# A 128-row score product with the forget bias in the free half of the key remainder

## The reference, cut to what matters

```python
log_f = jax.nn.log_sigmoid(f_logits.astype(jnp.float32) + b_f.astype(jnp.float32))
F = jnp.cumsum(log_f, axis=1).transpose(0, 2, 1)
s = jnp.einsum('bqhd,bkhd->bhqk', qc, k).astype(jnp.float32) * scale
s = s + Fq[..., None] - F[:, :, None, :]
```

## Time and profile before

| | |
|---|---|
| median of three runs | 1847.43 us |
| span of the profiled execution (first to last instruction) | 1849.7 us |
| busy: PE, DVE, ACT, POOL | 96%, 57%, 47%, 8% of the span |
| mean granted TensorE clock | 0.979 |

### The profile page before, as it was taken

How to read it: one execution, slowest core, us unless ns; L and a number is a source line. 1 busy time by engine, 2 the same in 40 slices (tenths; PEclk the granted TensorE clock), 3 DMA queues, 4 the chain that set the end, 5 groups by cost and what they waited for, 6 DMA issues and landing times.

```text
span 1849.7 us, 26742 instructions
## 1 busy us (share of the span) xinstructions
PE 1781.5 (96%) x8160; PEld 1344.1 (73%) x8160; DVE 1059.8 (57%) x2636; ACT 867.4 (47%) x1841; POOL 144.1 (8%) x170
## 2 busy tenths in 40 slices
PE   5999999999999999999969999999999999999997
PEld 3767777777777777888847777777777777688885
DVE  6467777765545555333465777777555554543344
ACT  3566666654444444222236666665444444432222
POOL 3121111100000000000023111111000000000000
PEclk8989999999999999999979999999999999999998
DMA  7220101012212123333432101011112221233331
GB/s 187 61 58 24 35 24 35 24 44 56 63 46 65 49 57 103 92 101 95 121 102 68 35 24 35 24 35 35 47 46 69 51 63 46 57 122 94 99 94 68
DMA packets 223875, 118.05 MB, mean 64 GB/s; under 512 B 20128, under 2 KB 220832, under 8 KB 223264
## 3 DMA queue, kind: packets, MB, share of 16 engines
q1 hardware_dynamic: 219104, 107.66, 21.8%
q0 software_dynamic: 1216, 8.65, 1.2%
q10 hardware_dynamic: 3456, 0.54, 0.2%
HBM read 110.41 MB, written 6.42 MB: 63 GB/s over the span
## 4 chain that ended last, share of the span: by engine, by line
PE 80%; ACT 7%; DVE 7%; issue 4%; POOL 1%; ACTq 1%; DVEq 0%; POOLq 0%
PE acc L1295 51%; PE o_pair L1381 9%; PE scores L1345 6%; PE turned L1358 5%; PE scores L1344 3%; ACT kk_hi L701 2%; PE scores L1349 2%; ACT w_hi L646 2%; ACT q_swap L682 1%; ACT prob L763 1%; DVE w_lo L929 1%; PE o_pair L1411 1%; PE misc L1396 1%; PE turned L1467 1%; DVE prob L1046 1%
## 5 line engine op out<-in xcount | busy, mean ns | idle before, releaser
L1295 PE MATMUL acc<-h_hi,w_hi 128*128 128x512 f32 (+1 forms) x1152 | 473.4, 411 | 30.0 <-DVE h_lo L431 24.1
L1295 PE MATMUL acc<-h_hi,w_lo 128*128 128x512 f32 (+1 forms) x1152 | 465.3, 404 | 0.0
L1295 PE MATMUL acc<-h_lo,w_hi 128*128 128x512 f32 (+1 forms) x1152 | 463.5, 402 | 0.0
L763 ACT ACTIVATE prob<-prob,row_max 128x128 f32<-128x128 f32 (+3 forms) x384 | 214.8, 559 | 270.1 <-DVE row_max L1027 268.1
L929 DVE TENSOR_TENSOR w_lo<-w_raw,w_hi 128x1024 fp32r<-128x1024 f32 x192 | 233.5, 1216 | 147.0 <-ACT w_hi L646 144.4
L1295 PEld LDWEIGHTS acc<-h_hi,w_hi 128*128 128x128 f32 (+1 forms) x1152 | 215.8, 187 | 101.8 <-DVE h_lo L431 29.4
L646 ACT ACTIVATE w_hi<-w_raw 128x1024 fp32r<-128x1024 f32 x192 | 199.7, 1040 | 180.2 <-PE acc L1295 176.1
L1295 PEld LDWEIGHTS acc<-h_hi,w_lo 128*128 128x128 f32 (+1 forms) x1152 | 216.1, 188 | 65.4 <-issue 21.4
L1295 PEld LDWEIGHTS acc<-h_lo,w_hi 128*128 128x128 f32 (+1 forms) x1152 | 216.3, 188 | 56.5 <-issue 16.1
L1027 DVE CUSTOM_DVE_ANT_0 prob<-scores,causal 128x128 f32<-128x128 f32 (+3 forms) x384 | 186.3, 485 | 118.3 <-PE scores L1349 55.0
L772 ACT ACTIVATE pt_hi<-turned 128x128 fp32r<-128x128 f32 (+3 forms) x384 | 165.1, 430 | 174.2 <-PE turned L1358 169.9
(11 more groups left out here) (156 smaller groups left out, 2066.4 us busy)
## 6 DMA issues: line engine op xcount, KB each, us to landing
w_raw<-in_w_in_dram SPq DMA_DIRECT2D x140, 512.0 KB, 3.8
w_raw<-in_w_proj_nsa_dram SPq DMA_DIRECT2D x16, 512.0 KB, 3.6
w_raw<-in_w_proj_fox_dram SPq DMA_DIRECT2D x16, 512.0 KB, 3.6
w_raw<-in_w_out_dram SPq DMA_DIRECT2D x16, 512.0 KB, 3.5
x_scratch<-xT POOLq DMA_DIRECT2D x2, 2048.0 KB, 9.2
xT<-x_scratch POOLq DMA_DIRECT2D x2, 2048.0 KB, 8.2
x_nat<-in_x_dram SPq DMA_DIRECT2D x2, 1024.0 KB, 6.7
c_w<-in_cmp_w_k_dram SPq DMA_DIRECT2D x4, 512.0 KB, 7.6
```

The lines of the kernel that those rows point to most:

```text
L763: act.activation(prob[:, ring, 0:width], prob[:, ring, 0:width], ACT.Exp, bias=row_max[:, ring:ring + 1], scale=-1.0, accum_out=row_sum[:, ...
L1295: ins = pe.matmul(acc[par][0:width, :], w[:, par, k, 0:width], rhs, start=(n == 0), stop=(n == 23))
```

## The change

`q_st` gets one more axis of two: index 0 is as before; index 1 is for fox and holds the rounded query in `own(h)` and, in `other(h)`, two rows of ones and 62 rows of zeros. `kk_lo[other(h)]` holds for fox the two bias rows and zeros. The second score matmul then has 128 rows: for fox index 1 by all of `kk_lo`; for NSA index 0, the same weights as the first, by all of `kk_lo`. The third matmul, `sel`, `sel_f` and `f_row` go. `q_round` writes the rounded fox query twice with one instruction. POOL clears the free half of `kk_lo` at the change from NSA to fox, once per buffer and layer, and fetches two rows per head with a transfer each. The ones and zeros of `q_st` are written once, at the start; so `q_st` moves to a place that nothing else overlays.

```diff
-        sel_f = sb("sel_f", [36, 2, P])
-        sel = sb("sel", [36, 2, P], F32R)
+        q_st = sb("q_st", [P, 2, 2, 2, T], F32R)
...
-            q_st = sb("q_st", [P, 2, 2, T], F32R)
+            sb("place_of_c_hid", [P, 4, T])
...
-            f_row = sb("f_row", [36, T], F32R)
...
-            pool.memset(sel_f[:, :, :], 1.0).then_inc(consts, 1)
+            pool.memset(q_st[:, :, :, 1, :].rearrange("p b h t -> p (b h) t").bitcast(F32), 0.0).then_inc(consts, 1)
...
-            for b in range(2):
-                rows = sel_f[32 * b:32 * b + 4]
...
+            for h in range(2):
+                first = HD * (1 - h)
+                pool.wait_ge(consts, 9 + h)
+                pool.memset(q_st[first:first + 2, :, h, 1, :].bitcast(F32), 1.0).then_inc(consts, 1)
...
-                    pool.dma_start(f_row[32 * proj.b:32 * proj.b + 4, :],
-                                   f_dram[bass.ds(2 * proj.i, 2)].rearrange("h a t -> (h a) t")
-                                   ).then_inc(f_landed, 16)
+                    if prev.nsa:
+
+                        if att.nsa:
+                            pool.wait_ge(cmp_pool, 3 * (att.l * PAIRS + att.i) + 3)
+                            apart(pool)
+                        for h in range(2):
+                            pool.memset(kk_lo[other(h), proj.b, h, :].bitcast(F32), 0.0).then_inc(bias_rows, 1)
+                        pool.wait_ge(bias_rows, 4 * l + 2 * proj.b + 2)
+                        apart(pool)
+                    for h in range(2):
+                        first = HD * (1 - h)
+                        pool.dma_start(kk_lo[first:first + 2, proj.b, h, :],
+                                       f_dram[bass.ds(2 * proj.i + h, 1)].rearrange("h a t -> (h a) t")
+                                       ).then_inc(f_landed, 16)
...
+                    if with_bias:
+                        ins = act.activation(q_st[own(h), b, h, :, :],
+                                             src[own(h), :].unsqueeze(1).broadcast_to([HD, 2, T]), ACT.Copy)
+                    else:
+                        ins = act.activation(q_st[own(h), b, h, 0, :], src[own(h), :], ACT.Copy)
...
-                    pe.matmul(to, q_st[:, pair.b, h, cols], kk_hi[:, b, stream, 0:n], start=True, stop=False)
-                    ins = pe.matmul(to, q_st[own(h), pair.b, h, cols], kk_lo[own(h), b, stream, 0:n], start=False,
-                                    stop=branch is not None)
-                    if branch is None:
-                        rows = slice(32 * b, 32 * b + 4)
-                        ins = pe.matmul(to, sel[rows, h, :], f_row[rows, 0:n], start=False, stop=True)
+                    pe.matmul(to, q_st[:, pair.b, h, 0, cols], kk_hi[:, b, stream, 0:n], start=True, stop=False)
+                    ins = pe.matmul(to, q_st[:, pair.b, h, 1 if branch is None else 0, cols],
+                                    kk_lo[:, b, stream, 0:n], start=False, stop=True)
```

More of the change, by code:

```diff
@@ L370, in bass_trunk @@
         z_done = sem("z_done")
-        sel_done = sem("sel_done")
+        bias_rows = sem("bias_rows")
         y_mul = sem("y_mul")
@@ L389, in bass_trunk @@
         kv_widths = [w for _, w in KV_UNITS]
-        N_CONSTS = 14
+        N_CONSTS = 12
         def apart(eng):
@@ L537, in _ @@
                                channel_multiplier=1).then_inc(consts, 1)
-            for b in range(2):
-                rows = sel_f[32 * b:32 * b + 4]
[L541 to L546, removed]
+            for h in range(2):
+                first = HD * (1 - h)
+                pool.wait_ge(consts, 9 + h)
+                pool.memset(q_st[first:first + 2, :, h, 1, :].bitcast(F32), 1.0).then_inc(consts, 1)
+            pool.wait_ge(consts, 11)
             pool.affine_select(out=past_first[:, :], in_=past_first[:, :], compare_op=ALU.is_ge, fill=0.0,
@@ L684, in swap_copy, with q_round @@
                     ins.then_inc(swap_done, 1)
-            def q_round(src, b, waits, heads=(0, 1)):
+            def q_round(src, b, waits, heads=(0, 1), with_bias=False):
                 for s, value in waits:
@@ L690, in q_round @@
                 for h in heads:
-                    ins = act.activation(q_st[own(h), b, h, :], src[own(h), :], ACT.Copy)
+                    if with_bias:
[3 more added lines that the diff above has]
+                        ins = act.activation(q_st[own(h), b, h, 0, :], src[own(h), :], ACT.Copy)
                 if 1 in heads:
@@ L752, in body @@
                         v_waits = [(cmp_s, PAIRS * (l + 1))] if att.nsa else [(v_turned, n)]
-                        at(plan.at_end(0, 1), lambda: q_round(acc[0], proj.b, q_waits))
+                        at(plan.at_end(0, 1), lambda: q_round(acc[0], proj.b, q_waits, with_bias=True))
                         at(plan.at_end(1, 1), lambda: k_round(acc[1], places, k_waits))
@@ L970, in q_rest @@
                 for h in range(2):
-                    ins = dve.tensor_tensor(q_st[other(h), b, h, :], src[own(h), :], q_st[own(h), b, h, :],
+                    ins = dve.tensor_tensor(q_st[other(h), b, h, 0, :], src[own(h), :], q_st[own(h), b, h, 0, :],
                                             ALU.subtract)
@@ L1112, in _ @@
             dve.wait_ge(consts, N_CONSTS)
-            dve.tensor_copy(sel[:, :, :], sel_f[:, :, :]).then_inc(sel_done, 1)
             for k in range(KT):
@@ L1339, in score_step @@
                         if not pair.nsa:
-                            pe.wait_ge(f_landed, 16 * (pair.l * PAIRS + pair.i + 1))
+                            pe.wait_ge(f_landed, 32 * (pair.l * PAIRS + pair.i + 1))
                     if s >= 2 or prev is not None or pair is not att:
@@ L1449, in _ @@
                 ins.then_inc(x_turned, 1)
-            pe.wait_ge(sel_done, 1)
             sum_squares(0)
```

## The result

The changed kernel takes 1718.6 us, median of four runs (1717.1 to 1719.5); the kernel before took 1848.7 us on the same chip. The ratio is 0.9304 [0.9289, 0.9320]. The profiled execution has a span of 1717.8 us, 131.9 less than before.

What follows compares the result with a forecast made beforehand. PE's matmuls were taken as the bound, with DVE's 28.7 us as floor of an NSA body. Fox 63 + 9 and NSA 46 + 11 gave 129 us off 1847.4: 1718 us, own range 1703 to 1738, wider range 1680 to 1766.

Steps and rivals of the forecast that it cites:

- The price of a step: PE time saved per score step: 0.39 us in NSA; 0.69, 0.76 or 0.83 us in fox for 256, 384, 512 columns.
- The fox body: Saves 5.94 us on PE, loses 1.45 in slots 4 and 5, so gains 4.5, to about 33.1 us.
- The NSA body: Saves 6.24 us on PE but gains 3.3 after waits, mostly for DVE, to about 34.3 us.
- slots 8 to 12: NSA stretch where the chain runs through ACT and DVE and keeps its length: four steps, 1.56 us, gain nothing.
- slots 4 to 6: NSA slots where DVE also has gated output and compressed-branch sums between its steps: estimated 0.9 us late.
- The mixed bodies: Two NSA bodies that project fox queries: PE stays their bound, 6.5 us gain at most, 5.5 taken each.
- The last fox bodies: Two bodies with seven score steps and a chain on PE alone: 5.25 us each at most, 4.5 taken.
- What was added: Wider `q_round`, POOL's transfers and memsets, later constants: nothing; worst cases 16 us, 59 us and 2.4 us respectively.
- the rival on the clock: Longer PE waits bring the granted clock to 1.2 GHz in each body: slower, 1956 us at half a body; chance 0.04.
- The rival with the load exposed: The second score matmul's weight load stays unhidden, so only the bias matmul's cost goes: 35 us, 1812 us; chance 0.08.
- The one without new lateness: Only the two stretches that leave PE now cost something: 152 us gained, 1695 us; chance 0.14.
- the one in which DVE takes all of NSA's gain: NSA bodies stay near 37.6 us; only fox and the two mixed bodies gain: 83 us, 1764 us; chance 0.19.

Runs made afterwards that it cites:

- second profile of before: The kernel before, unchanged, run and profiled once more: 1845.1 us, span 1843.5 us.
- NSA alone: The kernel before with only NSA's second score matmul at 128 rows, fox keeping its 64-row and bias matmuls: 1789.9 us, ratio 0.9694.

## Why the prediction was right, point by point

| term | predicted | measured |
|---|---|---|
| 14 regular NSA bodies | 14 x 3.3 = 46 | 12 x 3.37 + 2 x 1.94 = 44.3 |
| 14 regular fox bodies | 14 x 4.5 = 63 | 14 x 4.49 = 62.9 |
| two mixed NSA bodies | 2 x 5.5 = 11 | 2 x 4.15 = 8.3 |
| two last fox bodies | 2 x 4.5 = 9 | 2 x 5.04 = 10.1 |
| start, POOL, `q_round` | 0 | 0 |
| sum | 129 | 125.6 |

The first three rows are distances from the first score matmul of a pair to that of the next pair, in the second profile of before and in that of the changed kernel.

The difference of spans is 125.7 us against the second profile of before, 131.9 against the first, and 130.1 between the medians; single executions of one kernel differ by that much. The bodies gave 3 us less than the sum, and the median of the kernel before is 1.3 us above the one that the forecast started from: that 1718 met 1718.6 so closely is luck.

**The price of a step** was right, and it carries the result: 0.38 us for the two changes of height where 0.39 stood. It had been read from the kernel before as "exposed loads"; the runs add that the cause is the change of height. One sign that was named for it did not show: in the timeline of PE the second score matmul starts 0.20, 0.26 and 0.31 us behind the first for 256, 384 and 512 columns (medians; 0.29, 0.35 and 0.41 before), not 0.12, 0.18 and 0.23. Those distances stand one place later, from the second score matmul to the projection (0.12, 0.18 and 0.23; 0.31, 0.37 and 0.43 before). The first score matmul starts only 0.03 us behind the last transpose, and 0.03 + 0.20 + 0.12 is what the chain gives to a transpose and two score matmuls (0.11 + 0.12 + 0.12), so the saving of the step is not touched by it.

**The fox body** was right by its own steps: 33.1 us, the saving of slots 4 and 5 lost, and a wait of 1.75 us at unit 3 (about 1.9 foretold). The run with the earlier remainder shows that the order on DVE behind this wait held the body.

**The NSA body** came out at the size foretold (34.08 to 34.47 us, about 34.3 foretold), but its lateness lies partly elsewhere. The waits are those of the body in the window above. For slots 8 to 12 I had 1.56; PE waits 0.69 + 0.81 = 1.50 there. For the end of the body I had 0.5, behind the gate product; it is 0.58 at the first score of the next pair, which waits for `q_rest` on DVE (a place that I had not named), and 0.27 behind the gate product. For slots 4 to 6 I had 0.9; it is 0.17. The first of these was worked out and held; the other two were estimates, one too small and one too large, 1.02 together where 1.4 stood. That the body came out right is partly luck: the five waits make 2.52 of the 3.04 us that this body loses of 6.24 (it gained 37.60 - 34.40 = 3.20), and the rest, which may be the restarts behind them, no run separates. The first NSA body of each layer, counted among the 14, gains 1.94 us only (33.20 to 31.27 us in layer 1): PE waits there 1.40, 0.71 and 0.81 us for DVE's `pt_lo`, where the second profile of before has 0.26 and 0.20.

**The mixed bodies** gain 4.15 where I took 5.5. That PE stays their bound did not hold: in the one of layer 1 PE waits 0.69 and 1.08 us for DVE's `pt_lo` (357.28 and 369.98 us), where the second profile of before has one wait of 0.31. **The last fox bodies** gain 5.04, near the ceiling of 5.25: short slots cost them less than I took. Their four groups of value matmuls lie 27.4 us apart from first to last before (679.89 to 707.33) and 22.4 after (618.28 to 640.68).

**What was added** costs nothing, as foretold: the wider rounding is covered by the run with one copy, the later constants by the run with the late start, with the worst cases of 16 and 2.4 us not met; and in the list of PE's waits none is for the bias transfers.

**The rivals.** In the bodies the clock stayed at 1.00 despite the new waits, so the rival on the clock fell. The rival with the load exposed would have left the fox body near 35.48 us, as without the bias matmul; it takes 33.10. The one without new lateness (1695) fell to the waits behind the gate product and at the next pair's first score, and the one in which DVE takes all of NSA's gain to an NSA body of 34.35 us with NSA alone.

## What to carry to other kernels

Price a small matmul by the heights of its neighbours: one of 64 rows among matmuls of 128 cost its columns and about 0.4 us more for the change and the way back, and one of 4 rows behind it 0.31 us where its columns would take 0.12. Filling the unused rows (with zeros, or with a term that wants adding anyway) was worth 7% here. When PE becomes faster, first look for the stretches in which the chain already leaves it: what is saved beside them is lost, and moving one or two instructions to an earlier place in another engine's order may give it back (2.4% here, with no work taken away).

## What the runs showed that was not expected

The cost of a short matmul lies in the change of height: two neighbours of 64 rows on the same rows hide the second's load (0.12 us more for 256 columns), as neighbours of 128 rows do. The granted clock of one early stretch was 0.51 in one execution of the kernel before and 1.00 in another, and the two spans differ by 6.2 us: a single profile must not be taken for the price of anything below that. ACT's copy of 64 x 1024 takes 1015 ns where 64 x 512 took 585, so that, if the second half costs what the first does by its columns, 155 ns of the smaller one do not go by its columns.
